# Trainium2: the RWKV matrices of a hybrid decoder trunk as 64-wide chunk blocks, both token halves in step

## The reference, cut to what matters

```
def step(state, inp):                                   # state: (heads, 64, 64)
    r_t, w_t, k_t, v_t, a_t, b_t = inp
    sa = einsum('bhvk,bhk->bhv', state, a_t)
    state = state * w_t + sa[..., None] * b_t + v_t[..., None] * k_t
    return state, einsum('bhvk,bhk->bhv', state, r_t)   # a = -kk, b = kk * a_gate
```

## Time and profile before

| what | value |
|---|---|
| median of 3 runs | 1655.37 us (1653.63 to 1662.83) |
| the profiled execution | 1655.44 us, its span 1653.6 us |
| TensorE busy | 1494.6 us, 90% of the span |
| VectorE, ScalarE, GpSimd busy | 1056.8, 653.1, 234.0 us |
| DMA | 298.28 MB, 180 GB/s over the span |
| granted TensorE clock, mean | 0.950 of 2.4 GHz |

### The profile page before, as it was taken

How to read it: one execution, slowest core, us unless ns; L and a number is a source line. 1 busy time by engine, 2 the same in 40 slices (tenths; PEclk the granted TensorE clock), 3 DMA queues, 4 the chain that set the end, 5 groups by cost and what they waited for, 6 DMA issues and landing times.

```text
span 1653.6 us, 29105 instructions
## 1 busy us (share of the span) xinstructions
PE 1494.6 (90%) x12001; PEld 1442.1 (87%) x12001; DVE 1056.8 (64%) x1383; ACT 653.1 (39%) x941; POOL 234.0 (14%) x258
## 2 busy tenths in 40 slices
PE   3799998876889998999989999888678999899997
PEld 3799998865779998999989999887567899899997
DVE  5777667555544667676677766755564466767754
ACT  2433334546112435433343333554521243543333
POOL 2122200110210000232003320002011100012300
PEclk9799999987999999999999999988879999999999
DMA  8989786541002845998669888664200095589861
GB/s 278 303 268 275 261 275 160 143 116 26 1 1 63 259 159 147 273 267 272 227 191 281 264 288 263 169 162 117 62 1 1 1 251 196 153 233 280 266 219 46
DMA packets 352786, 298.28 MB, mean 180 GB/s; under 512 B 19736, under 2 KB 295217, under 8 KB 352561
## 3 DMA queue, kind: packets, MB, share of 16 engines
q1 hardware_dynamic: 352688, 296.96, 60.2%
HBM read 295.88 MB, written 1.05 MB: 180 GB/s over the span
## 4 chain that ended last, share of the span: by engine, by line
PE 82%; DVE 9%; ACT 4%; DVEq 1%; issue 1%; DMA 1%; ACTq 1%; SPq 0%
PE PS L1392 21%; PE PS L1394 21%; PE PS L1393 21%; PE PS L1463 2%; DVE ada_acc L923 2%; DVE wl L839 2%; PE PS L1792 2%; PE PS L1781 2%; PE PS L1790 1%; ACT wh L539 1%; PE PS L1454 1%; PE PS L1748 1%; DVE PS L852 1%; DMA x_rows<-in_x 1%; PE PS L1679 1%
## 5 line engine op out<-in xcount | busy, mean ns | idle before, releaser
L1392 PE MATMUL PS<-h_hi,wh 128*128 128x256 f32 x2256 | 644.2, 286 | 38.9 <-DVE h_lo L861 28.2
L839 DVE TENSOR_TENSOR wl<-raw,wh 128x1024 fp32r<-128x1024 f32 (+1 forms) x400 | 472.2, 1221 | 303.5 <-ACT wh L539 303.4
L539 ACT ACTIVATE wh<-raw 128x1024 fp32r<-128x1024 f32 (+1 forms) x400 | 396.0, 1039 | 620.7 <-PE PS L1394 614.3
L1393 PE MATMUL PS<-h_lo,wh 128*128 128x256 f32 x2256 | 637.9, 283 | 0.0
L1394 PE MATMUL PS<-h_hi,wl 128*128 128x256 f32 x2256 | 637.1, 282 | 0.0
L1392 PEld LDWEIGHTS PS<-h_hi,wh 128*128 128x128 f32 x2256 | 435.6, 193 | 42.6 <-issue 36.3
L1393 PEld LDWEIGHTS PS<-h_lo,wh 128*128 128x128 f32 x2256 | 437.1, 194 | 0.1
L1394 PEld LDWEIGHTS PS<-h_hi,wl 128*128 128x128 f32 x2256 | 434.8, 193 | 0.0
L923 DVE SCALAR_TENSOR_TENSOR ada_acc<-ada_w_ring,cact,ada_acc 128x512 f32<-128x512 f32 x280 | 219.0, 782 | 24.4 <-issue 1.8
L1392 PE MATMUL PS<-hid_hi,wh 128*128 (+1 forms) x704 | 198.8, 282 | 0.0
L1394 PE MATMUL PS<-hid_hi,wl 128*128 (+1 forms) x704 | 198.5, 282 | 0.0
(11 more groups left out here) (288 smaller groups left out, 1688.0 us busy)
## 6 DMA issues: line engine op xcount, KB each, us to landing
raw<-in_ffn_w_in SPq DMA_DIRECT2D x176, 512.0 KB, 5.4
ada_w_ring<-in_ada_w SPq DMA_DIRECT2D x160, 512.0 KB, 5.0
raw<-in_mix_w_in SPq DMA_DIRECT2D x90, 512.0 KB, 6.4
raw<-in_ffn_w_out SPq DMA_DIRECT2D x44, 1024.0 KB, 5.7
raw<-in_branch_w SPq DMA_DIRECT2D x8, 1024.0 KB, 5.4
raw<-in_mix_w_out SPq DMA_DIRECT2D x8, 1024.0 KB, 4.8
raw<-in_mix_w_in SPq DMA_DIRECT2D x2, 1024.0 KB, 6.9
cst<-in_consts SPq DMA_DIRECT2D x1, 1216.0 KB, 5.4
```

The lines of the kernel that those rows point to most:

```text
L539: nc.scalar.activation(wh[:, s % 2, h * n:(h + 1) * n], raw[:, s % 4, h * n:(h + 1) * n], ACT.Copy).then_inc(*one("w_hi"))
L839: V.tensor_tensor(wl[:, s % 2, h * n:(h + 1) * n], raw[:, s % 4, h * n:(h + 1) * n], wh[:, s % 2, h * n:(h + 1) * n].bitcast(F32), ALU.sub ...
L1392: M(out, wh[(slice(None),) + wsl], rhs_h, start=start, stop=False, skip_group_check=True)
L1393: M(out, wh[(slice(None),) + wsl], rhs_l, start=False, stop=False, skip_group_check=True)
```

## The change

1. **Blocks of 64.** The matrices are kept as 64-wide blocks: chunk 0 of a half on partitions 0 to 63, chunk 1 on partitions 64 to 127, [128, par, 3, 64], so 384 elements a partition in place of 768. Every matmul of the stage has 64 rows, 64 columns and a moving operand of 64 elements. With `q` the chunk, `chunk_mm` writes from partitions 64q.. to PSUM partitions 64q.. (the tiles on the array's corners), both into the same bank.
2. **Both halves together.** First everything is built for tt=0 and tt=1, in seven steps each that take turns on two pairs of PSUM banks; each step waits until the one two before it is copied out. Then each doubling `b` runs for both halves, and these two form the pipeline that the two `par` halves formed before. G, wT and u0 follow for both halves, and then one chain over the four chunks.
3. **State per head.** S is [128, 3, 64] with no blocks of zeros; `pcm` and GpSimd's work for it are gone, VectorE multiplies by the decay itself. u0 is accumulated in PSUM and not copied out and added; the output is copied out per chunk by ScalarE.
4. **Who copies.** ScalarE copies all transposes, two PSUM banks at a time, and G; VectorE keeps the masks, the sums and u.
5. **Constants and places.** The masks shrink from nine of 128 columns to ten of 64; `cst` goes from 19 x 128 to 10 x 128 + 10 x 64 columns. The shared region now begins at 64 modulo 512 bytes.

The core of the diff:

```diff
         base = nc.sbuf_base
-        base = (base + 511) // 512 * 512
+        base = (base + 511 - 64) // 512 * 512 + 64
@@ ScalarE
+                    for i in range(2):
+                        act.wait_ge(*at("tok_done", 2 * tt + i + 1, l))
+                        p = 2 * ((7 * tt + i) % 2)
+                        nc.scalar.activation(tok[tt][:, 2 * i:2 * i + 2, :], PS[:, p:p + 2, 0:BW], ACT.Copy)
+                for b in range(5):
+                    for tt in range(TT):
+                        act.wait_ge(*at("z_done", 2 * b + tt + 1, l))
+                        nc.scalar.activation(Z[tt]..., PS[:, Z_BANKS[tt], 0:BW], ACT.Copy)
...
@@ VectorE
                 for tt in range(TT):
+                    for i, (dst, msk) in enumerate(((AT, K_UP), (Tm, K_LO1), (Aak, K_UP), (Arb, K_UPI), (Ark, K_UPI))):
+                        dve.wait_ge(*at("ab_done", 5 * tt + i + 1, l))
+                        V.tensor_tensor(dst[tt], both(7 * tt + 2 + i), chunk_mask(msk), ALU.mult)
+                        if i == 1:
+                            dve.drain()
+                            V.tensor_tensor(Tm[tt], Tm[tt], chunk_mask(K_ID), ALU.add)
+                            V.tensor_tensor(TTm[tt], AT[tt], chunk_mask(K_UP1), ALU.mult)
+                            dve.drain()
+                            V.tensor_tensor(TTm[tt], TTm[tt], chunk_mask(K_ID), ALU.add).then_inc(*one("T_ready"))
+                for b in range(5):
+                    for tt in range(TT):
+                        dve.wait_ge(*at("tz_done", 2 * b + tt + 1, l))
+                        if b < 4:
+                            V.tensor_tensor(tm, tm, PS[:, 2 * tt, 0:BW], ALU.add)
+                        V.tensor_tensor(ttm, ttm, PS[:, 2 * tt + 1, 0:BW], ALU.add).then_inc(*one("T_ready"))
+                for ch in range(4):
+                    dve.wait_ge(*at("u_done", ch + 1, l))
+                    V.tensor_copy(u_[tt][rows]..., PS[rows, 2 * tt:2 * tt + 2, 0:BW // 2])
...
+                    V.tensor_tensor(S, S, PS[:, S_BANK, 0:BW // 2]..., ALU.add)
                     dve.drain()
+                    V.tensor_tensor(S, S, cum[:, :, end:end + 1].broadcast_to([P, 3, CHUNK]), ALU.mult)
@@ GpSimd
-                        G.tensor_tensor(pcm[:, :, :], const(C_BLK)..., cum[...]..., ALU.mult)
+                        G.tensor_tensor(X[tt], AT[tt], chunk_mask(LEVELS[b]), ALU.mult)
@@ TensorE
+                def product(n, lhs, rhs):
+                    step_free(n - 2)
+                    for c in range(3):
+                        for q in range(2):
+                            for par in range(2):
+                                ins = M(PS[half(q), 2 * (n % 2) + par, c * 64:c * 64 + 64], lhs[half(par), c, ts],
+                                        rhs[half(par), c, ts], start=True, stop=True)
+                def chunk_mm(b, lhs, rhs):
+                    for c, par, _, _ in heads_of():
+                        o = (3 * par + c) * 64
+                        for q in range(2):
+                            ins = M(PS[half(q), b, o:o + 64], lhs[half(q), par, c, :], rhs[half(q), par, c, :],
                                     start=True, stop=True)
+                for b in range(5):
+                    for tt in range(TT):
+                        pe.wait_ge(*at("X_ready", 2 * b + tt + 1, l))
+                        pe.wait_ge(*at("T_ready", 2 * b + tt + 1, l))
+                        chunk_mm(Z_BANKS[tt], X[tt], Tm[tt]).then_inc(*one("z_done"))
+                    for tt in range(TT):
+                        pe.wait_ge(*at("z_ready", 2 * b + tt + 1, l))
+                        if b < 4:
+                            chunk_mm(2 * tt, TTm[tt], Z[tt])
+                        chunk_mm(2 * tt + 1, Z[tt], TTm[tt]).then_inc(*one("tz_done"))
...
+                for ch in range(4):
+                    for c, par, _, r in heads_of():      # u, onto u0 in PSUM
+                        ins = M(PS[half(q), 2 * tt + par, c * 64:c * 64 + 64], wT[tt][r, q, c, :], S[r, c, :],
+                                start=False, stop=True, skip_group_check=True)
+                    for c, par, _, r in heads_of():      # S.r, opens the output of the chunk
+                        ins = M(PS[r, Y_BANK, c * 64:c * 64 + 64], S[r, c, :], rr[r, c, ts], start=(c == 0), stop=False, ...)
+                    for c, par, hc, r in heads_of() if ch < 3 else ():
+                        M(PS[r, S_BANK, c * 64:c * 64 + 64], tok[tt][half(q), 2, hc], tok[tt][half(q), 3, hc], ...)
+                    pe.wait_ge(*at("u_ready", ch + 1, l))
...
```

More of the change, by code:

```diff
@@ L103, in shape_constants @@
     same = (r // CHUNK) == (c // CHUNK)
[L104 to L107, removed]
+    out = [np.eye(P), np.ones((P, P)), same, r >= c, r < c, np.where(r < c, 0.0, NEG), np.where(c <= r, 0.0, NEG)]
     reset = np.ones((P, T))
@@ L150 @@
 NORM_BANK = (3, 3, 4, 3)
+Z_BANKS, S_BANK, Y_BANK = (4, 7), 4, 7
 def hybrid_trunk(nc, a, per_layer, tally):
@@ L764, in _ @@
                 for tt in range(TT):
[L765 to L772, removed]
@@ L1148, in _ @@
                 for tt in range(TT):
[L1149 to L1155, removed]
@@ new lines, in half, with step_free, turn @@
+                def half(q):
+                    return slice(64 * q, 64 * q + 64)
+                def step_free(n):
+                    tt, i = n // 7, n % 7
+                    pe.wait_ge(*(at("tok_ready", 2 * tt + i + 1, l) if i < 2 else at("a_ready", 5 * tt + i - 1, l)))
+                def turn(n, srcs):
+                    ts = slice(n // 7 * P, n // 7 * P + P)
+                    if n >= 2:
+                        step_free(n - 2)
+                    for i, src in enumerate(srcs):
+                        for c in range(3):
+                            ins = nc.tensor.transpose(PS[:, 2 * (n % 2) + i, c * P:(c + 1) * P], src[:, c, ts], ident)
+                    ins.then_inc(*one("tok_done"))
@@ L1755, in _ @@
-                    pe.wait_ge(*at("S_ready", 2 * tt + 1, l))
-                    for i, src in enumerate((kk, av, kp, vv)):
-                        for c in range(3):
-                            ins = nc.tensor.transpose(PS[:, i, c * P:(c + 1) * P], src[:, c, ts], ident)
-                    ins.then_inc(*one("tok_done"))
-                    A(4, av, kk, tt, "ab_done")
-                    if tt:
-                        pe.wait_ge(*at("ya_ready", tt, l))
+                    n = 7 * tt
+                    turn(n, (kk, av))
@@ L1795, in _ @@
[L1795 to L1803 removed]
+                    turn(n + 1, (kp, vv))
@@ new lines, in _ @@
+                pe.wait_ge(*at("tok_ready", 4, l))
+                for tt in range(TT):
+                    for c, par, hc, _ in heads_of():
+                        o = (3 * par + c) * 64
+                        for q in range(2):
+                            ins = M(PS[half(q), Z_BANKS[tt], o:o + 64], Aak[tt][half(q), par, c, :], tok[tt][half(q), 3, hc],
+                                    start=True, stop=True)
+                    ins.then_inc(*one("g_done"))
+                for tt in range(TT):
+                    pe.wait_ge(*at("T_ready", 10 + tt + 1, l))
+                    for c in range(3):
+                        for q in range(2):
+                            for par in range(2):
+                                hc = slice((2 * c + par) * 64, (2 * c + par) * 64 + 64)
+                                ins = M(PS[half(par), 2 * tt + q, c * 64:c * 64 + 64], tok[tt][half(q), 0, hc],
+                                        TTm[tt][half(q), par, c, :], start=True, stop=True)
@@ L1827, in _ @@
[L1827 to L1833 removed]
+                    pe.wait_ge(*at("wt_ready", tt + 1, l))
```

260 lines of the change are left out of this document (114 added, 146 removed).

## The result

The changed kernel takes 1557.62 us (median of 5 runs, 1549.57 to 1560.12) against 1660.96 for the kernel before in 5 runs (1653.63 to 1662.83): a ratio of **0.9374, 95% interval 0.9346 to 0.9401**. The profiled execution took 1549.57 us, the fastest of the five, its span 1547.8: 105.8 less than the 1653.6 of before; by the medians it is 103.3 less.

A forecast was written before the change was run, and what follows sets the result against it. TensorE was taken to bound the kernel. The stage's parts summed to 54.0 us against 96.3, 84.6 saved in all; 1655.4 - 84.6 - 4 (shift) - 1.0 (constants) = 1566 us, range 1552 to 1617.

The forecast's parts named there:

- The price of a pass: RWKV stage: a pass of 64 rows, 64 columns, 64 moving elements costs 0.028 us with two corner tiles side by side.
- Rival 3: RWKV stage: an issue limit puts a pass at 0.040 us, stage 63, kernel 1584 us; chance 0.13.
- rival 4: RWKV stage: turns and half clock together, or a small pass at full cost, 0.111 us; kernel 1760 us; chance 0.04.
- Rival 1: RWKV stage: corner tiles take turns, a pass is 0.055 us, kernel 1617 us; chance 0.20 together with rival 2.
- Build: First part of the new stage, transposes and masked products for both halves: 15.1 us, set by VectorE.
- Inversion: The doublings of the stage, both halves together: 22.1 us, 4.81 for each doubling b = 1 to 3.
- G, wT, u0: Stage, after the inversion: 6 groups of 24 passes, 4.0, plus 0.2 wait for wT's copy: 4.2 us.
- Chain: Last part of the stage, four chunks: 10.6 us, 2.7 for each of three and 2.5 for the last.
- Clock: Stage: 2 us kept for TensorE running at the lower clock level, since VectorE's gaps remain in the new build.
- Rival 2: Stage: the clock stays at half level with quarter-array tiles and gaps, kernel 1620 us; chance 0.20 together with rival 1.
- The shift: Shared SBUF region moved to 64 modulo 512 bytes, hid and y matmuls: -4 us, between -20 and +3.
- Constants: Kernel start: 256 KB less loaded ahead of x, which the first transposes wait for: -1.0 us.

The follow-up runs named there:

- the blocks of the corner-tile order: Changed kernel with `chunk_mm` issuing the 12 passes of one corner tile, then the 12 of the other, instead of taking turns: 1594.09 us in one run.
- the repeat: The changed kernel run once more, unaltered, on the chip of the later versions: 1557.2 us (6 runs), ratio 0.9346 to the kernel before.

## Why the prediction came out right

**The price of a pass, 0.028, measured 0.030.** The step that carried all: halving the width and the moving operand together halves the period of a tile (0.057 on one tile, from the blocks of the corner-tile order; forecast 0.055), where halving the moving operand alone had left it at 0.107, and two tiles side by side halve it again. Rival 3 (0.040) is out, and so is rival 4. Rival 1 had the shared bank for it: the Trainium skill, "TensorEngine Tiling (Array Packing)", Restrictions and Gotchas, says that different row tiles can't access one PSUM bank at the same time. For corner tiles, which differ in rows and in columns, the measurement decides against it: two of them start within 15 ns into one bank, and the pass is 0.030, not 0.055. Tiles that differ in rows alone and share a bank were not tried.

**Build, 15.1, measured 13.1.** The mis-sized term is the product: I priced it with two tiles at work, 0.67, but its loops run over `par` (rows) and `q` (columns), all four tiles, and it takes 23 x 0.016 = 0.36. Two products lie on the path of each half, 0.6 of the 1.0 us a half. Of the rest, 0.2 are the three dependent steps of Tm and TTm, 1.9 for 2.1: the first, beside GpSimd, takes 0.70 where the others take 0.54 and 0.56. That VectorE sets the build's time holds: moving its dependent steps back shortens the build by 3.4 us.

**Inversion, 22.1, measured 450.95 - 428.06 = 22.9.** A doubling is 4.92 for 4.81: TensorE issues 144 x 0.030 = 4.3 and waits 0.6, where I had 4.03 and 0.78. **G, wT, u0, 4.2, measured** 455.17 - 450.95 = 4.2. **Chain, 10.6, measured** 465.78 - 455.17 = 10.6, a chunk 2.69 for 2.7.

**Clock, +2 a layer, measured 0** in the changed kernel's profile; in the repeat, layer 0 was 1.5 us longer at 0.77 in the build. The term belongs to an execution, not to the kernel: with the same build the clock fell in 9 of 16 stages and cost 0.3 to 2 us there. The profiled execution was the fastest of the five, with the highest mean clock (0.963, the others 0.954 to 0.958), so 0 is its lucky end. The cause that I named, VectorE's gaps, is not settled: the clock fell in each of twelve waits of 3.3 to 4.5 us and held in the two of 2.62, but with waits of 1.6 to 1.8 it did either. Rival 2 was nearer than its chance said: the corner tiles do lose the clock where one half's waits lie open (0.63, stage 81.3), and on one layer of two where the tiles don't alternate (0.50). "Both halves together" buys the clock as well as the waits; the forecast had the second and took the first for granted.

**The shift, -4, measured -9.1.** The place was the cause, which the forecast left open because h_hi's own stretch also showed 54 in 20 us. Both ways round, region back at 0 and shift alone in the kernel before, hid and y change by 7 to 8 and by 1 us. The -20 came from counting matmuls in windows, 0.357 against 0.333 for three; the spacing itself is 0.357 against 0.340 at best, which makes at most 14. And `h_hi` "slow at times" is its second value: in the window from 88 of the earlier trace rows all its groups take 0.353, in that from 624 all take 0.340. The size is well inside -20 to +3, and its upper end among executions.

**Constants, -1.0, measured -0.1.** The step failed: the constants land earlier (4.8 us after their issue for 5.4), but x_rows do not. The first matmul on the constants starts at 5.77 us (6.59 before), while the transposes of x_rows, the row that answers to the earlier trace rows, start at 15.47 against 15.53:

```profile
5.77 0.45 PE L1518 MATMUL PS<-cst,vrows 128*128 128x128 f32 x1 [5.77 <-DMA vrows<-in_final_norm_g]
...
15.47 1.75 PE L1524 MATMUL PS<-cst,x_rows 128*128 128x128 f32 x7 [9.26 <-DMA x_rows<-in_x]
```

The wait for x_rows is 9.26, up from 8.49: what was saved ahead of it turned into wait. What x's own load waits for was not tried.

**Sum.** Stage 91.6 for 84.6 (build 2 x 2, clock 2 x 2, less 0.8 x 2 in the inversion; the layer-1 stage 0.5 better still), shift 9.1 for 4, constants 0.1 for 1.0. The other 4.6, in the h_hi stretches, lie within what these stretches vary by: in the profiles of variants and repeat they are 966.0 to 978.6. I take them for chance. So the forecast was right for its mechanism, while its number was low in what it saves: 89.6 forecast, 103.3 by the medians. Only 8 us of that show between 1566 and 1557.6, because the forecast started from 1655.4 and the kernel before came out at 1660.96 in more runs. That what follows the stage might wait for loads did not come: the gain is whole at the end.

## What to carry to other kernels

Small block-diagonal products belong on corner tiles, with consecutive matmuls on different tiles: then a 64 x 64 x 64 product in fp32 costs 0.030 us a pass, and 0.016 over four tiles. Interleave two independent dependent chains not only for their waits but for TensorE's clock, and where no second chain exists, try idle matmuls in the gaps: they took 1613 to 1597 us here. A gain of some us in its own stretch can be hidden in the total, because the clock or the spacing moved elsewhere; compare stretch by stretch, over several profiles.

## What the hardware showed that I had not expected

- The clock can stay at 1.2 GHz while TensorE is busy in 20.00 of 20 us, in blocks on one 64 x 64 tile at a time; the same code on the other layer had 2.4 GHz.
- How far apart tiles can overlap depends on order: in blocks of 12 the next tile starts only some three passes ahead of the end, and 24 passes take 1.04 us in place of 0.70.
- A moving operand at 64 modulo 512 bytes makes three 256-element matmuls 0.340 or 0.353 us, in blocks that follow each other, in place of 0.357 with it at 0 or 256: 5 to 8 us over 704 groups. Why is open; no other offset was tried.
- One and the same build, with waits of 1.6 to 1.8 us, kept 2.4 GHz in 7 of 16 stages and lost it in 9, up to 2 us each.
